# Twelve modulation pieces summed on three engines beside the first layer's projection, and the recurrence's preparation reordered

## The chip, the cores and the metric

The kernel runs on one core of one Trainium2 chip. The metric is the device time of one execution in microseconds; of the kernel before, three runs are known, with a median of 3143.65 us (3140.86 to 8241.34). The profile is of one further execution.

## What is computed

A two-layer hybrid diffusion backbone: 1024 latent tokens and 256 context tokens, width 1024, float32. Each layer first makes six modulation vectors for the latent and six for the context tokens out of two conditioning vectors:

```python
mod_l = silu(c)     @ w_ada[layer] + b_ada[layer]      # w_ada: (2, 1024, 6144)
mod_c = silu(c_ctx) @ w_ada[layer] + b_ada[layer]
sh1, sc1, g1, sh2, sc2, g2 = split(mod, 6)
h = rms_norm(x) * (1 + sc1) + sh1                      # both streams
layer 0:  z = h @ w_in; grouped attention beside a bidirectional chunkwise mLSTM; @ w_out
layer 1:  differential attention beside latent attention; @ w_out
each layer: x = x + g1 * mixer(h);  x = x + g2 * moe(rms_norm(x) * (1 + sc2) + sh2)
```

For the change only the products with `w_ada` matter. The matrix has 24 column pieces of 512 (NCHUNK), each 1024 x 512, 2 MB. A product of a vector with a piece is the sum over 1024 rows, that is over k = 0 to 7 (eight row blocks of 128, a row on each partition) and over the 128 partitions.

## The kernel before, in words

The stages follow one another; each is a block in which every engine and the DMA queue of SyncE has its own hand-written list, ordered by semaphores.

`modulation` makes the first four pieces (EARLY), which the first normalisation needs, on TensorE (`ada_product`, L152). `even_attend` and later stages make the last eight (LAST). The twelve between are the subject. Six of them (SUMMED = 6) are reduced over k, though not over the partitions, inside `even_project`; the other six are loaded whole, 2 MB each, in `even_mlstm`.

`even_project` (L366) walks ten tiles of 128 tokens, two tiles to a pair i, h = 0 or 1. A tile's order on TensorE (`tile`, L523): `rows` groups 0 and 1, `turn_qk` of the tile before, `rows` group 2, `transposes` of the tile after, `rows` group 3, `channels` in two halves. `turn_qk` waits for `x_sq` (ScalarE's squares at the end of the tile before) and for `z_dve`. `transposes` waits for the normalised x of the next tile (`xh_ready`) and for `qt_act` and `qt_dve`, the copies of the turned queries and keys out of PSUM; the latter is `k_out` on VectorE, which stands behind `rows_out`. VectorE's tile: `summed` half 0, `rows_out`, `k_out`, `norm_rope`, `modulate`, `summed` half 1, `channels_out`, `normalise` for the tile after next. ScalarE's tile: `rows_out`, `q_out`, `v_out`, `modulate`, `gate_out`, `channels_out`, `squares`.

`summed` (L679) takes one piece per tile, in tiles 1 to 6, with both conditioning vectors ("kinds"): SyncE loads the piece in two slabs of 1 MB into the last 512 columns of zT, VectorE multiplies each block k by a per-partition scalar and adds it to one of two accumulators in the last columns of qT, 16 instructions in all, where the two kinds alternate so that an instruction waits for the one before the last. `acc_store` writes both accumulators to `sum_dram`; the next piece waits for that store. GpSimd only fills `y_dram` with zeros (18.9 MB, L453), once the last part of the weights is in.

`even_mlstm` (L741) prepares the recurrence and then runs it. The preparation: SyncE loads eight units of up to 2 MB over four buffers (sums of pieces 0 to 3, three whole pieces, sums of 4 and 5, three whole pieces); TensorE reduces each (`product`), ScalarE copies it (`ada_out`), TensorE turns it (`turn`). Between them runs the chain of the gates: cumulated sums, an 18-step running maximum on one partition, two scans (L1131), exponentials; and the eight channel gates, a tanh on ScalarE (`gate`, L1029) and a product of 128x1280 on VectorE (`gated`, L1080), for which two buffers alternate. GpSimd stages each chunk of the recurrence (L902 to L908); its first staging waits for all eight channel gates, for the gate tables, for the rows loaded from `row_dram` and for the buffers that the loads of `w_ada` hold. TensorE's `scores` waits for that staging.

Of the kernel before, what the change touches and what calls it, by code (L numbers as in the profile page):

```python
# [144 lines left out]
SUMMED = 6  # L145
# [213 lines left out]

def modulation_of(g, layer, i, h, k):  # L360

    kind = 1 if isinstance(i, int) and i == 0 else 0
    return g.gain[:, layer, 0, k:k + 1, kind], g.mod[:, layer * 48 + V_SH1 * KD + k:layer * 48 + V_SH1 * KD + k + 1, kind]


def even_project(nc, g, A, L):  # L366
# [5 lines left out]
    with nc.cleanup_on_exit():  # L372
# [31 lines left out]
        acc = [L.qT[:, kind, T - 512:T] for kind in range(2)]  # L404
        slab_in, slab_used = [s("slab_in0"), s("slab_in1")], [s("slab_used0"), s("slab_used1")]
        acc_st = s("acc_st")
        c = Count(nc, "ep_dve_step")
        with nc.Block() as block:

            @block.sync  # L410
            def _(sp):
# [5 lines left out]
                def slab_load(n, half):  # L417
                    if n:
                        sp.wait_ge(slab_used[half], n)
                    col = (EARLY + n) * 512  # L420
                    sp.dma_start(slabs[:, 4 * half:4 * half + 4, :],
                                 A["w_ada"][0, half * 512:(half + 1) * 512, col:col + 512].rearrange("(k p) n -> p k n", p=P)).then_inc(slab_in[half], 16)

                def acc_store(n):
                    sp.wait_ge(slab_used[1], n + 1)
                    sp.dma_start(g.sum_dram[:, n, :, :], L.qT[:, 0:2, T - 512:T]).then_inc(acc_st, 16)
# [6 lines left out]
                x_load(1)  # L433
                for n in range(SUMMED):
                    if n + 1 < SUMMED:
                        slab_load(n + 1, 0)
                    x_load(n + 2)
                    acc_store(n)
                    if n + 1 < SUMMED:
                        slab_load(n + 1, 1)  # L440
                for n in range(SUMMED + 2, NTL):
                    x_load(n)
                sp.wait_ge(acc_st, 16 * SUMMED)

            @block.gpsimd
            def _(pool):
# [3 lines left out]
                pool.wait_ge(L.w_in[2], 16)  # L450
# [88 lines left out]
            def _(act):  # L539
# [38 lines left out]
                def channels_out(i, h, halves=(0, 1)):  # L578

                    if h == 0 and not place_of(i, h)[0] and not place_of(i, h)[1]:  # L580
                        act.wait_ge(slab_used[1], i * 2)
# [7 lines left out]
                def q_out(i, h):  # L589
                    if h == 0 and not place_of(i, h)[0] and not place_of(i, h)[1]:  # L590
                        act.wait_ge(acc_st, i * 32)
# [7 lines left out]
                def tile(i, h):  # L599
                    first, final, last, before, after = place_of(i, h)  # L600
                    rows_out(i, h)
                    if not first:
                        q_out(*before)
                    v_out(i, h)
                    if not last:
                        modulate(*after)
                    gate_out(i, h)
                    if last:
# [3 lines left out]
                    else:  # L612
                        channels_out(i, h)
                    if not final:
# [4 lines left out]
                walk_tiles(act, tile)  # L619
# [3 lines left out]
            def _(dve):  # L623
# [16 lines left out]
                def rows_out(i, h):  # L640
                    dve.wait_ge(r_done, i * 8 + 4 * h + 2)
                    dve.tensor_copy(qk[:, AW:QK], ps_r[:, 1, 0:AKW]).then_inc(*c.up())
# [36 lines left out]
                def summed(i, h, half):  # L679

                    n = i * 2 + h - 1
                    dve.wait_ge(slab_in[half], n * 16 + 16)
                    if half == 0 and not (isinstance(n, int) and n == 0):
                        dve.wait_ge(acc_st, n * 16)
                    for k in range(4 * half, 4 * half + 4):
                        for kind in range(2):
                            by = L.cs[:, k, kind:kind + 1]
# [2574 lines left out]
```

## Time and profile before

| | us |
|---|---|
| median of 3 runs | 3143.65 |
| the profiled execution | 3144.81 |
| its span, first to last instruction | 3142.90 |
| `modulation` | 0 to about 36 |
| `even_project` | about 36 to 447 |
| `even_mlstm`, preparation | 447 to 495 |
| recurrence | 495 to 600 |
| busy TensorE / VectorE / ScalarE / GpSimd | 2876.6 / 1481.4 / 1083.3 / 693.0 |

Times in a timeline are in us from the start of the span. A row has the start, the duration, the engine, the line of the kernel, the operation, output and inputs and the count of merged instructions; what stands in brackets is the engine's idle time before it and what ended that. PEclk is the granted TensorE clock, where 1.00 is 2.4 GHz and 0.50 is 1.2 GHz.

### The profile page before, as it was taken

The page shows a single profiled execution, that of the slowest core. Times are in us where ns is not written, and L with a number is a line of the kernel's source. Part 1 is how long each engine was busy: PE and PEld are TensorE (multiplying, and loading weights), DVE is VectorE, ACT ScalarE, POOL GpSimd, SP SyncE. Part 2 cuts the span into 40 slices and gives each one's busy share as a digit, 9 for nine tenths or more (in the row PEclk, how much of TensorE's full clock was granted, in tenths as well). Part 3 has the DMA queues.
Part 4 walks back from the last instruction along what each step waited for, and adds up shares of the span by engine and source line. Part 5 has one row for each costly group of instructions (what it writes and reads, how often), then busy time and mean ns, then how long its engine had stood idle before and what let it go on. Part 6 is the DMA issues. An engine that isn't in the chain of part 4 may idle for free. (4 is left out here: it accounts for less than half of the span.)

```text
span 3142.9 us, 72871 instructions
## 1 busy us (share of the span) xinstructions
PE 2876.6 (92%) x27771; PEld 1881.7 (60%) x27771; DVE 1481.4 (47%) x4244; ACT 1083.3 (34%) x2480; POOL 693.0 (22%) x929
## 2 busy tenths in 40 slices
PE   7999978899999689999987999899999959998895
PEld 4666657655544357776664555477776537785563
DVE  2666436755554522222224677666665342222223
ACT  1211224466611123333333443455553103332232
POOL 0000005798050033332221010000002013332233
PEclk8999988899999899999998999999999979998898
DMA  9822037432052499999984221200003459999997
GB/s 376 291 77 85 14 121 217 114 109 93 1 183 94 176 373 416 410 416 417 418 336 158 85 83 61 74 1 1 1 1 123 148 223 396 417 417 417 418 416 289
DMA packets 167396, 665.00 MB, mean 212 GB/s; under 512 B 25372, under 2 KB 37928, under 8 KB 117620
## 3 DMA queue, kind: packets, MB, share of 16 engines
q1 hardware_dynamic: 136736, 574.30, 47.1%
q0 software_dynamic: 19456, 56.67, 5.1%
q10 hardware_dynamic: 10964, 30.68, 2.6%
q8 instruction: 170, 2.79, 0.4%
q14 instruction: 70, 0.57, 0.1%
HBM read 581.98 MB, written 86.90 MB: 213 GB/s over the span
## 5 line engine op out<-in xcount | busy, mean ns | idle before, releaser
L2879 PE MATMUL ps_g<-w_ring,work 128*32 128x256 f32 x7328 | 434.7, 384 | 26.6 <-DMA w_ring<-in_w 15.1
L2966 DVE STREAM_TRANSPOSE work<-work 128x256 f32<-128x256 f32 x189 | 123.8, 655 | 660.9 <-PE ps_g L2879 638.1
L2932 ACT COPY work<-ps_y 32x256 f32<-32x256 f32 x760 | 275.8, 363 | 289.7 <-PE ps_y L2894 282.9
L2879 PEld LDWEIGHTS ps_g<-w_ring,work 128*32 128x32 f32 x7328 | 285.6, 111 | 144.9 <-issue 33.5
L2879 PE MATMUL ps_g<-w_early,work 128*32 128x256 f32 x4640 | 283.1, 390 | 30.8 <-DMA w_early<-in_w 19.8
L2004 PE MATMUL of_ps_r<-w_early,cat 128*128 128x512 f32 (+1 forms) x608 | 257.2, 579 | 1.6 <-ACT cat L2086 1.6
L486 PE MATMUL ps_r<-w,hT 128*128 128x512 f32 (+1 forms) x640 | 250.2, 547 | 1.5 <-ACT hT L556 1.5
L2879 PEld LDWEIGHTS ps_g<-w_early,work 128*32 128x32 f32 x4640 | 181.6, 112 | 111.7 <-issue 41.9
L2827 POOL DMA_INDIRECT work<-f_dram,ex_idx x200 | 204.5, 1023 | 171.4 <-POOL ex_idx L2824 170.6
L2894 PE MATMUL ps_y<-w_ring,work 128*32 128x256 f32 x3680 | 228.0, 382 | 3.9 <-ACT work L2932 3.4
L2926 ACT ACTIVATE work<-ps_g 128x128 f32<-128x128 f32 x192 | 53.2, 277 | 514.1 <-PE ps_g L2879 507.6
L2835 POOL COPY work<-work 128x256 f32<-128x256 f32 x192 | 76.6, 399 | 539.4 <-DVE work L2966 398.2
L2004 PEld LDWEIGHTS of_ps_r<-w_early,cat 128*128 128x128 f32 x608 | 115.2, 193 | 125.4 <-issue 123.2
L486 PEld LDWEIGHTS ps_r<-w,hT 128*128 128x128 f32 x640 | 120.5, 192 | 114.9 <-issue 107.5
L1655 PE MATMUL mo_ps_o<-mo_w,mo_cT 128*128 128x512 f32 x416 | 185.0, 596 | 1.4 <-DMA mo_w<-in_e_w_out 0.9
L2894 PEld LDWEIGHTS ps_y<-w_ring,work 128*32 128x32 f32 x3680 | 147.0, 111 | 61.2 <-ACT work L2932 4.3
L2466 DVE TENSOR_SCALAR_CACHE_REDUCE w_early<-oa_ps_s 128x512 f32<-128x512 f32 (+1 forms) x288 | 158.9, 598 | 20.3 <-PE oa_ps_s L2380 17.6
L2435 ACT ACTIVATE w_early<-w_early,oa_mins 128x1280 f32<-128x1280 f32 x96 | 131.0, 1364 | 66.1 <-DVE oa_mins L2472 66.1
L497 PEld LDWEIGHTS ps_ab<-hT,w 128*128 128x128 f32 x1280 | 144.6, 192 | 4.8 <-issue 4.8
L497 PE MATMUL ps_ab<-hT,w 128*128 128x128 f32 x1280 | 144.7, 275 | 0.0
L2894 PE MATMUL ps_y<-w_early,work 128*32 128x256 f32 x2304 | 144.6, 387 | 0.0
L1655 PEld LDWEIGHTS mo_ps_o<-mo_w,mo_cT 128*128 128x128 f32 x416 | 78.6, 191 | 99.7 <-issue 97.5
(509 smaller groups left out, 4441.0 us busy)
## 6 DMA issues: line engine op xcount, KB each, us to landing
w_ring<-in_w SPq DMA_DIRECT2D x232, 1024.0 KB, 25.3
w_early<-in_w SPq DMA_DIRECT2D x152, 1024.0 KB, 25.2
y_dram<-work ACTq DMA_DIRECT2D x190, 128.0 KB, 5.9
y_dram<-zeros POOLq DMA_DIRECT2D x4, 4608.0 KB, 26.8
ea_slab<-in_w_ada SPq DMA_DIRECT2D x64, 256.0 KB, 2.8
zT<-in_w_ada SPq DMA_DIRECT2D x12, 1024.0 KB, 6.5
f_dram<-mo_f SPq DMA_DIRECT2D x18, 512.0 KB, 2.9
w<-in_e_w_in SPq DMA_DIRECT2D x2, 4096.0 KB, 20.9
```

The lines of the kernel that those rows point to most:

```text
L486: mm = pe.matmul(ps_r[:, n, 0:cols[1] - cols[0]], hT[:, h, k, :], w[:, k, cols[0]:cols[1]], start=k == 0, stop=k == KD - 1)
L497: mm = pe.matmul(ps_ab[:, h, half, (cc % 4) * P:(cc % 4) * P + P], w[:, k, Z0 + cc * P:Z0 + (cc + 1) * P], hT[:, h, k, :], start=k == 0, s ...
L1655: mm = pe.matmul(ps_o[:, half * 512:(half + 1) * 512], row, w[:, k, half * 512:(half + 1) * 512], start=k == 0, stop=k == KD - 1)
L2004: mm = pe.matmul(ps_r[:, bank[m], 0:b - a], hT[:, n % 2, k, :], w[:, k, a:b], start=k == 0, stop=k == KD - 1)
L2435: act.activation(sx[:, n % 3, part, :], sx[:, n % 3, part, :], ACT.Exp, scale=-1.0, bias=mins[:, n % 3, part, 3:4], accum_out=sums[:, n % ...
L2466: dve.tensor_scalar(sx[:, n % 3, part, a:b], ps_s[:, k % 2, part, 0:b - a], -SCALE[units[n][1]], BIG, ALU.mult, ALU.min, accum_out=mins[:, ...
L2827: pool.indirect_dma_start(out=xg[:, at * 256:(at + 1) * 256], out_offset=None, in_=R.f_dram.rearrange("t (q d) -> (t q) d", q=QU), in_offs ...
L2835: pool.tensor_copy(xs, xg[:, at * 256:(at + 1) * 256]).then_inc(x_ready, 1)
L2879: mm = pe.matmul(ps_h[rows, :], xT[:, k * UNIT:(k + 1) * UNIT], w[:, :, kk * DE + n * P:kk * DE + (n + 1) * P], start=k == 0, stop=k == KD ...
L2894: mm = pe.matmul(ps_y[n * UNIT:(n + 1) * UNIT, :], hT[:, k * UNIT:(k + 1) * UNIT], w[:, kk, n * 256:(n + 1) * 256], start=k == 0, stop=k == 3)
L2932: w = act.copy(y[b * UNIT:(b + 1) * UNIT, n * 256:(n + 1) * 256], ps_y[n * UNIT:(n + 1) * UNIT, :])
L2966: dve.transpose(xT.rearrange("p (k t) -> p k t", k=KD), xs.rearrange("p (r k) -> p k r", k=KD)).then_inc(x_turned, 1)
```

## The change

All twelve middle pieces are summed in `even_project` (SUMMED = 12), two to a tile, in tiles 0 to 5. VectorE accumulates kind 0 alone, 8 instructions a piece, each of which waits for the one before. For kind 1 ScalarE multiplies (`weighed`, with a scale on each partition) into a ring of four products, which lie in the last columns of qT, kT and v, and GpSimd adds them up, seven adds a piece. ScalarE waits for GpSimd where the ring is full; GpSimd waits for the store of the sum before. The zeros of `y_dram` are now issued after GpSimd's last add. The second piece of tile 0 lies behind its `channels_out` and ahead of `squares` and `normalise`.

In `even_mlstm` three units of four summed pieces take the place of the eight. The preparation's order changes: the loads of the values come ahead of those of the rows, `gated(0)` and `gated(1)` move behind the scans, the clearing of `hb` is done at once (the tanh buffer that lay in it moves to `third`), and the copies of the products stand elsewhere among ScalarE's gates.

```diff
-SUMMED = 6
+SUMMED = 12
@@ even_project, SyncE
                 def slab_load(n, half):
                     if n:
-                        sp.wait_ge(slab_used[half], n)
+                        sp.wait_ge(used_dve[half], n)
+                        sp.wait_ge(product_made, 8 * n - 4 + 4 * half)
...
+                def sum_store(n):
+                    sp.wait_ge(used_dve[1], n + 1)
+                    sp.dma_start(g.sum_dram[:, n, 0, :], acc).then_inc(dve_st, 16)
+                    sp.wait_ge(product_added, 7 * n + 7)
+                    sp.dma_start(g.sum_dram[:, n, 1, :], acc_pool).then_inc(pool_st, 16)
...
                 for n in range(SUMMED):
+                    slab_load(n + 1, 0)
+                    slab_load(n + 1, 1)
+                    sum_store(n)
+                    if n % 2 == 0:
+                        x_load(n // 2 + 1)
@@ GpSimd
-                pool.wait_ge(L.w_in[2], 16)
+                for n in range(SUMMED):
+                    for k in range(1, 8):
+                        pool.wait_ge(product_made, 8 * n + k + 1)
+                        if n and k == 1:
+                            pool.wait_ge(pool_st, 16 * n)
+                        if n or k > 1:
+                            pool.wait_ge(product_added, 7 * n + k - 1)
+                        pool.tensor_tensor(acc_pool, product[0] if k == 1 else acc_pool, product[k % 4], ALU.add).then_inc(product_added, 1)
@@ ScalarE
+                def weighed(n, half):
+                    act.wait_ge(slab_in[half], n * 16 + 16)
+                    for k in range(4 * half, 4 * half + 4):
+                        if half:
+                            act.wait_ge(product_added, n * 7 + max(k - 4, 1))
+                        elif not (isinstance(n, int) and n == 0):
+                            act.wait_ge(product_added, n * 7 - 3 + k)
+                        act.activation(product[k % 4], slabs[:, k, :], ACT.Copy, scale=L.cs[:, k, 1:2]).then_inc(product_made, 1)
                 def tile(i, h):
+                    if sums and not first:
+                        weighed(n, 0)
                     rows_out(i, h)
                     if not first:
                         q_out(*before)
+                    if sums and not first:
+                        weighed(n, 1)
...
                     gate_out(i, h)
+                    if sums:
+                        for half in range(2):
+                            weighed(n if first else n + 1, half)
...
+                    if first:
+                        for half in range(2):
+                            weighed(1, half)
                     if not final:
                         squares(i + 1, h)
@@ VectorE
-                                dve.wait_ge(*c.but(1))
+                                dve.wait_ge(*c.now())
...
-                    if sums:
-                        summed(i, h, 0)
+                    if sums and not first:
+                        summed(n)
                     rows_out(i, h)
...
                     if sums:
-                        summed(i, h, 1)
+                        summed(n if first else n + 1)
                     channels_out(i, h)
+                    if first:
+                        summed(1)
@@ even_mlstm
+        units = [(4 * n, 4 * n + 4) for n in range(SUMMED // 4)]
@@ SyncE
-                        rows_in(0, step)
-                        rows_in(1, step)
-                        sp.wait_ge(ada_mm, LATE - 1)
                         for b in range(4):
                             values_in(b, tiles)
+                        sp.wait_ge(rows_out, 32)
+                        rows_in(0, step)
+                        rows_in(1, step)
@@ ScalarE
-                for cc in range(2, 8):
-                    gate(cc)
-                    if cc < 6:
-                        ada_out(cc)
-                for n in range(6, LATE):
-                    ada_out(n)
+                gate(2)
+                ada_out(2)
+                for cc in range(3, 8):
+                    gate(cc)
```

## Rows read from the trace of the kernel before

**Rows 1.** Windows: length, busy PE, PEld, DVE, ACT, POOL, then PEclk, DMA share, GB/s
```profile
130.00:170.00 40.00, 40.00 (x207) 27.80 (x206) 26.28 (x71) 7.95 (x19) 0.00 (x0) 1.00 0.36 123
...
447.00:500.00 53.00, 37.81 (x210) 17.53 (x211) 22.25 (x64) 19.22 (x27) 12.16 (x16) 0.69 0.99 346
```
**Rows 2.** Timeline of TensorE in tiles 1 to 3 of the projection
```profile
100.41 1.04 PE L469 MATMUL ps_ab<-consts_sb,x 128*128 128x128 f32 x8
...
122.44 10.70 PE L486 MATMUL ps_r<-w,hT 128*128 128x512 f32 x32
...
140.39 1.04 PE L469 MATMUL ps_ab<-consts_sb,x 128*128 128x128 f32 x8
...
162.42 10.70 PE L486 MATMUL ps_r<-w,hT 128*128 128x512 f32 x32
```
**Rows 3.** Timeline of VectorE in tile 2, which starts at 122.44
```profile
127.86 0.15 DVE L628 TENSOR_SCALAR xs<-xs 128x1 f32<-128x1 f32 x1 [1.27 <-ACT ps_ab L548]
...
130.10 0.88 DVE L689 TENSOR_SCALAR qT<-zT,cs 128x512 f32<-128x512 f32 x2
...
135.71 0.29 DVE L699 COPY kT<-ps_ab 128x128 f32 x1
...
145.80 5.38 DVE L692 SCALAR_TENSOR_TENSOR qT<-zT,cs,qT 128x512 f32<-128x512 f32 x8
157.20 0.30 DVE L667 COPY edges<-ps_ab 128x4 f32 x2 [6.02 <-ACT zT L585]
```
**Rows 4.** Timeline of ScalarE in tile 2
```profile
126.68 1.03 ACT L548 ACTIVATE ps_ab<-x 128x1024 f32<-128x1024 f32 x1 [2.54 <-DVE zT L675]
...
133.82 0.59 ACT L593 COPY qT<-ps_ab 128x512 f32 x1 [3.63 <-PE ps_ab L517]
```
**Rows 5.** GpSimd's adds of the same size in the attention stage, grouped by line
```profile
L1319 POOL TENSOR_TENSOR ea_slab<-ea_slab 128x512 f32<-128x512 f32 x56 | 71.3, 1273 | 4.7
```
**Rows 6.** Timeline of GpSimd at 883 us and in the recurrence
```profile
883.34 1.04 POOL L1610 TENSOR_TENSOR hb<-hb,mo_rs 128x512 f32<-128x512 f32 x1 [106.39 <-DVEq L1795]
884.46 3.20 POOL L1612 TENSOR_TENSOR hb<-hb,gbc 128x512 f32<-128x512 f32 x1
...
530.46 1.26 POOL L908 TENSOR_TENSOR ml_staging<-zT,ml_arena 128x512 f32<-128x512 f32 x1
```
**Rows 7.** Timeline of VectorE at 883 us and in the recurrence
```profile
883.36 3.18 DVE L1787 TENSOR_TENSOR mo_sq<-hb 128x2048 f32<-128x2048 f32 x1
...
530.55 1.18 DVE L1195 TENSOR_TENSOR ml_dn<-ml_dn,ml_cur 128x4 f32<-128x4 f32 x1
...
549.66 0.16 DVE L1195 TENSOR_TENSOR ml_dn<-ml_dn,ml_cur 128x4 f32<-128x4 f32 x1
```
**Rows 8.** DMA issues by line: KB each, median us from issue to landing
```profile
zT<-in_w_ada SPq DMA_DIRECT2D x12, 1024.0 KB, 6.5
...
sum_dram<-qT SPq DMA_DIRECT2D x6, 512.0 KB, 3.2
```
**Rows 9.** Windows of 2 us after stretches in which TensorE stood
```profile
44.00:46.00 2.00, 2.00 (x3) 0.67 (x2) 0.00 (x0) 0.00 (x0) 0.00 (x0) 0.54 0.99 397
...
456.00:458.00 2.00, 2.00 (x12) 0.44 (x12) 1.65 (x11) 0.00 (x0) 0.00 (x0) 0.50 1.04 396
...
492.00:494.00 2.00, 0.49 (x4) 0.20 (x8) 0.00 (x0) 0.00 (x0) 0.20 (x1) 0.74 1.01 267
```
**Rows 10.** Timeline of TensorE in the preparation
```profile
455.85 3.38 PE L924 MATMUL ml_ps_c<-ml_staging,ml_sel 128*32 128x512 f32 x16
...
493.51 3.32 PE L157 MATMUL ml_ps_c<-ml_arena,cs 128*32 128x512 f32 x16 [3.68 <-DMA ml_arena<-in_w_ada]
```
**Rows 11.** Timeline of VectorE in the preparation
```profile
459.47 0.15 DVE L1122 TENSOR_TENSOR ml_m_row<-ml_m_row 1x8 f32<-1x8 f32 x1
...
489.28 1.48 DVE L1080 SCALAR_TENSOR_TENSOR zT<-ml_spare,zT 128x1280 f32<-128x1280 f32 x1
```
**Rows 12.** Timeline of GpSimd: the first staging of the recurrence
```profile
494.97 0.20 POOL L902 COPY ml_cur<-ml_tab 128x16 f32<-128x16 f32 x1 [2.77 <-DMA ml_spare<-ml_rows]
```

More of the change, by code:

```diff
@@ L357, in place_of, with is_tile, has_sums @@
     return first, final, final and h == 1, (i, 0) if h else (i - 1, 1), (i + 1, 0) if h else (i, 1)
+def is_tile(i, h, n):
+    return isinstance(i, int) and i * 2 + h == n
+def has_sums(i, h):
+    return not (isinstance(i, int) and i * 2 + h >= SUMMED // 2)
 def modulation_of(g, layer, i, h, k):
@@ L578, in channels_out @@
                 def channels_out(i, h, halves=(0, 1)):
-                    if h == 0 and not place_of(i, h)[0] and not place_of(i, h)[1]:
-                        act.wait_ge(slab_used[1], i * 2)
+                    if is_tile(i, h, FREED):
+                        for half in range(2):
+                            act.wait_ge(used_dve[half], SUMMED)
                     for half in halves:
@@ L613, in tile @@
                         channels_out(i, h)
+                    if first:
+                        for half in range(2):
+                            weighed(1, half)
                     if not final:
@@ L618, in _ @@
                 modulate(0, 0)
-                walk_tiles(act, tile)
+                tile(0, 0)
+                tile(0, 1)
+                with act.Fori(0, FREED // 2 - 1) as j:
+                    tile(j + 1, 0)
+                    tile(j + 1, 1)
+                for i in range(FREED // 2, PAIRS):
+                    tile(i, 0)
+                    tile(i, 1)
                 act.wait_ge(vo_out, 16 * NT + 16)
@@ L702, in tile @@
                     first, final, last, before, after = place_of(i, h)
-                    sums = not first and not (isinstance(i, int) and i * 2 + h > SUMMED)
-                    if sums:
-                        summed(i, h, 0)
+                    sums, n = has_sums(i, h), i * 4 + 2 * h
+                    if sums and not first:
+                        summed(n)
                     rows_out(i, h)
@@ L765, in even_mlstm @@
         qs, ks, qa, tm = (staging[:, :, n, :, :] for n in range(4))
-        whole = EARLY + SUMMED
-        units = [("sums", 0, 4)] + [("whole", q) for q in range(whole, whole + 3)] + [("sums", 4, SUMMED)] + [("whole", q) for q in range(whole + 3, LAST[0])]
+        units = [(4 * n, 4 * n + 4) for n in range(SUMMED // 4)]
         LATE = len(units)
@@ L825, in _ @@
             def _(sp):
-                def load(n):
-                    if n >= len(wa):
-                        sp.wait_ge(ada_mm, n - len(wa) + 1)
-                    if units[n][0] == "sums":
-                        _, a, b = units[n]
-                        sp.dma_start(wa[buf(n)][:, 0:2 * (b - a), :], g.sum_dram[:, a:b, :, :].rearrange("p n w c -> p (n w) c")).then_inc(ada_in[buf(n)], 16)
-                    else:
-                        ada_load(sp, A, units[n][1], wa[buf(n)], ada_in[buf(n)])
-                for n in range(6):
-                    load(n)
+                for n, (a, b) in enumerate(units):
+                    sp.dma_start(wa[n], g.sum_dram[:, a:b, :, :].rearrange("p n w c -> p (n w) c")).then_inc(ada_in[n], 16)
                 sp.wait_ge(gd, 6)
@@ L841, in _ @@
                 sp.dma_start(row_dram[1].rearrange("d r t -> (d r) t"), ai_row).then_inc(rows_out, 16)
-                for n in range(6, LATE):
-                    load(n)
-                sp.wait_ge(rows_out, 32)
                 def rows_in(b, step):
@@ L964, in _ @@
                 pe.matmul(ps_s[:, 1, 0:P], g.ident[:, 0:1].to_broadcast([P, P]), ai_col, start=True, stop=True).then_inc(gp, 1)
+                turn(0)
+                product(2)
                 turn(1)
-                for n in range(3, LATE):
-                    product(n)
-                    turn(n - 1)
-                turn(LATE - 1)
+                turn(2)
                 def scores(u, b):
@@ L1137, in _ @@
                 dve.sem_inc(gd, 1)
+                gated(0)
                 dve.wait_ge(gp, 5)
```

132 lines of the change are left out of this document (58 added, 74 removed).

## The prediction

> **What bounds the kernel now.** I read the windows by stage first. In the projection TensorE is busy for 40.00 of 40.00 us at full clock, while VectorE has 26.3 us of work, ScalarE 8.0 and GpSimd none; in the preparation TensorE is busy 37.8 of 53 us at a mean clock of 0.69 and the DMA engines 0.99 of the time [rows 1]. So the projection is TensorE's and the preparation looks like the loads'. The second view is the timeline of each engine in one tile. TensorE starts a tile every 39.98 us (122.44, 162.42), and its transposes of the next x follow 17.95 us behind the start [rows 2]. Against these two marks everything that the change puts into a tile must be held. Third, the timelines of the preparation: the running maximum ends at 459.6 and the last channel gate at 490.8 [rows 11], GpSimd stages the first chunk at 494.97 [rows 12], and TensorE stands 3.7 us for the last whole piece [rows 10]. From GpSimd's start on, all later work only shifts.
>
> **The preparation: what is saved.** Before, 12 MB of whole pieces and 3 MB of sums went through four buffers; after, three units of 2.1 MB, each with a buffer of its own. At 396 GB/s [rows 9] from 448.5 the third lands at 448.5 + 3 x 5.3 = 464.4 (before, TensorE still waited for a load at 493.51). The chain that is left, step by step. The running maximum ends at 459.6 as before. Its turn into a column, a copy, two scans and their two ends took 2.2 us without the two channel gates that stood between them (2 x 1.48 less the little that they overlap); so the scans are done at 461.8. Then gated(0), 1.5, to 463.3; the small copies, 0.9, to 464.2; gated(1) to 465.7; copies and gated(2) to 467.6. ScalarE's gate(3) now stands behind the copy of the third unit: landing 464.4, TensorE free at about 466, a product of 3.4 us at half clock [rows 10], some 1.9 at full, copy 0.6, gate 1.3: 470 to 471.5. Five more products at a pitch of 1.45 (1.48 each on VectorE [rows 11], ScalarE one ahead) end at 477.2 to 478.7. The clearing of the tanh buffer (1.4 us) no longer stands between that and the staging. The rows of the tables are loaded behind 1 MB of values; their store goes out at 462.3, lands behind the third unit at about 467, and 1 MB of values and 1 MB of rows at 396 GB/s end at 473 to 476, ahead of the gates. GpSimd starts at 478.5 in place of 494.97: **16.5 us saved**, between 14 (rows land late, at 481) and 17.8 (full clock).
>
> **The projection without collisions.** Times in a tile are from its start on TensorE. The tile's first piece starts when x is normalised, 130.10 - 122.44 = 7.66 [rows 3]. Its eight chained instructions cost 0.48 and 7 x (0.745 + 0.035), 6.0 us; before, eight took 4.9. `rows_out` and `k_out` add 0.85: ready at 14.5, and the transposes want it at 17.95, a margin of 3.4 us. The second piece stands behind `modulate`, where 8 instructions took 5.38 and VectorE then waited 6.0 us for the channels [rows 3]. ScalarE gets 16 x 0.58 = 9.3 us beside its 8, and GpSimd 14 x 1.27 = 17.8 us [rows 5] of 40. Loads of 1 MB take 6.5 us and stores 3.2 [rows 8]; both pieces have over 8 us for it in tiles 2 to 5. The zeros, about 48 us at 396 GB/s, start at about 280 and are there long before 447. By busy time alone all of it lies beside TensorE. Only tile 1 is different: piece 1 stands behind `channels_out` of tile 0, so VectorE normalises x later, and piece 2 has to wait until the sum of piece 1 is stored. Without collisions VectorE ends piece 1 at 92.7, the 1 MB load and the store behind it land at 98 to 99, piece 2 takes 6.0, `k_out` 0.9: 105.2 against the transposes at 100.41 [rows 2], a stall of 4.8 us.
>
> **What the busy times hide: VectorE and GpSimd take turns.** In the trace VectorE's product of two SBUF tensors, 128x2048, starts at 883.36 beside GpSimd's 1.04 us product, and takes 3.18 us; GpSimd's next one starts at 884.46 and takes 3.20 us where 1.27 is its usual length: it ends 1.12 us behind VectorE's [rows 5 to 7]. In the recurrence a VectorE product of 128x4 lasts 1.18 us beside a GpSimd product (530.46 to 531.72, VectorE ends at 531.73), and 0.16 us when none runs [rows 6, 7]. So each stands until the other's instruction has ended, and they alternate. VectorE's multiply-adds here read two SBUF tensors (slab and accumulator), as do GpSimd's adds, so one pair costs 1.12 + 0.6 = 1.73 us, at most 1.27 + 0.78 = 2.05, in place of 0.78 for VectorE.
>
> The Trainium skill's page "SBUF — State Buffer" (section "Who interferes with whom") states this as a rule: a VectorE instruction with two SBUF inputs contends with a GpSimd instruction that reads SBUF, and the one that comes second blocks fully. It speaks against the split that this change makes; the trace agrees, with 1.18 against 0.16 us.
>
> *Tiles 2 to 5.* z_dve, where VectorE has copied the last channels of the tile before, is at 4.3. ScalarE's squares end at 5.4 (126.68 + 1.2 of its own tile) [rows 4], its products follow at 0.5 us each, and GpSimd's first add is ready at 6.8, in the midst of VectorE's normalisation. Adds 1 to 3 have their products at once; the fifth product stands behind the copy of the queries at 133.82, that is 11.4, so adds 4 to 7 come from 12.5 on [rows 4]. In order: add 1 to 8.05, add 2 to 9.2, the normalising product of x to 9.8, add 3 to 10.9, VectorE's first product to 11.3, multiply-adds 1 and 2 to 12.8, then four pairs to 19.7, the last multiply-add to 20.5, `rows_out` and `k_out` to 21.35. TensorE wants it at 17.95: a stall of 3.4 us. The second piece (behind `modulate` at about 31) pays the same seven collisions, 12.1 us in place of 6, and ends at about 45, which the wait for the channels (the channels' copies start at 34.8, [rows 3]) mostly hides; where it does not, the next tile starts 1.4 us later in its own time and the stall is 4.8. Such a stand also costs clock: the window of 44 to 46 us has 0.54, though TensorE had been at work since 40.1 without a stop, and the stand before 493.51, 3.7 us, was followed by 3.3 us at half clock [rows 9, 10]. Half clock for 3 to 6 us is 1.5 to 2.9 us. I take 5.4 us a tile, **21.6 us** for four. Bounds: 3.4 (no clock lost) and 11 (pairs of 2.05, full 8 us stall and 2.9 of clock), 13.6 and 44 us.
>
> *Tile 1.* Piece 1 alternates with its seven adds and ends at 98.3, not 92.7; load and store behind it land at 104 to 106; piece 2 with its seven pairs takes 0.45 + 12.1 and ends at about 117.6, `k_out` at 118.5: 18 us behind 100.41, and 2.9 of clock. **21 us**; bounds 16 and 25.
>
> **The sum.** +21.6 + 21 - 16.5 = +26 us on the profiled execution's 3144.8, so 3171; on the median of the runs shown, 1.2 us lower, 3170. A measurement of this kernel can tell about 2%, 63 us, from no change.
>
> **Rivals.**
> 1. *The two engines do not collide on these operands.* Then tile 1 costs 4.8 + 1.7 of clock and nothing else: 3143.7 + 6.5 - 16.5 = 3134, faster. For it: nothing in the trace but the durations of GpSimd's adds in the attention stage (1.27 throughout), where VectorE reads PSUM. Against it: both rows above. It decides at VectorE's first piece of a tile: below 9.4 us with no stall, above it TensorE waits. 15%.
> 2. *Collisions at the upper bounds.* Pairs of 2.05, both pieces of a tile late, so each tile starts with z_dve at 7.7 and stalls 8.3 us and loses 2.9 in clock: 4 x 11.2 + 25 - 16.5 = +53, 3197. For it: VectorE's busy 28 plus 17.8 us of adds, plus waits for squares and channels, come near 48 a tile. Against it: the overlaps of 0.13 us in the rows. 17%.
> 3. *The stage's gain is not there:* the gates' chain is bound by something that the loads hid, such as the rows landing behind the values at 486. Then 8 us are saved: 3178. Against it: 6 MB in place of 15. 5%.
> 4. Slower by over 63 us: with the queries' copy on ScalarE held by GpSimd as well, tile after tile. 4%.
>
> **Chances and range.** The forecast (net +10 to +42) has 59%. The range goes from rival 1's 3134 to rival 2's 3197. The likeliest case alone spans 3152 to 3186. Faster by over 2%: 1%; within 2%: 95%; slower: 4%.
>
> **What would show it.** Right: in tiles 2 to 5 TensorE stands 3 to 5 us ahead of L469's transposes for kT's copy, and once about 18 us in tile 1; VectorE's multiply-adds of 128x512 last 1.1 to 1.9 us in the mean instead of 0.745, and windows of 40 us show a granted clock below 1.00; the projection ends near 447 + 42 = 489 and the first staging comes 31 us after that, not 48. Wrong: multiply-adds of 0.75 us with GpSimd's adds beside them (rival 1), or a tile of 48 us and more (rival 2). The preparation is wrong where GpSimd's first staging waits for loaded rows, not for the last gate.

## The result and the profile after

| | before | after |
|---|---|---|
| median of 5 runs each, on one chip, us | 3140.86 | 3168.65 |
| the profiled execution's span, us | 3142.9 | 3165.3 |
| mean period of tiles 2 to 5, us | 39.98 | 45.87 |
| tile 1, us | 39.98 | 58.48 |
| start of `even_mlstm`, us | 447.41 | 490.88 |
| from there to the first staging, us | 47.56 | 30.18 |

The ratio after to before is 1.0094 with a 95% interval of 1.0072 to 1.0116: about 28 us slower, clear of noise, and within 2%. One of the five runs of the kernel before took 8241.34 us; its cause is not known and it is left out of the ratio. The projection grew by 43.5 us and the preparation gave 17.4 back; at the first staging the changed kernel is 26.1 us behind (494.97 in [rows 12] against 521.06). The later stages of these two profiled executions differ by 4 us the other way, which is less than the runs of one kernel differ among themselves (3163.05 to 3175.39).

What TensorE waits for in the projection, grouped by the instruction that waits (us in total, times, longest). The kernel before had no wait of this kind:

```profile
PE ps_ab L497 <- DVE kT L757: 30.5, 5, 16.3
```

L497 are the transposes of the next x (L469 before), L757 is `k_out` on VectorE. There are five stands (a stand is a stretch in which TensorE waits), one in each of tiles 1 to 5. TensorE's timeline in tiles 1 and 2:

```profile
83.57 10.70 PE L514 MATMUL ps_r<-w,hT 128*128 128x512 f32 x32
...
118.00 1.94 PE L497 MATMUL ps_ab<-consts_sb,x 128*128 128x128 f32 x8 [16.32 <-DVE kT L757]
119.73 8.19 PE L514 MATMUL ps_r<-w,hT 128*128 128x512 f32 x16
...
142.05 10.70 PE L514 MATMUL ps_r<-w,hT 128*128 128x512 f32 x32
...
163.53 1.94 PE L497 MATMUL ps_ab<-consts_sb,x 128*128 128x128 f32 x8 [3.37 <-DVE kT L757]
165.27 7.61 PE L514 MATMUL ps_r<-w,hT 128*128 128x512 f32 x16
```

Compare with [rows 2]. The transposes take 1.94 us in place of 1.04, and the 16 matmuls behind them, 7.03 us at full clock, take 7.6 to 8.2 here and up to 9.0 in tiles 3 to 5: the stand is paid a second time in clock. The stands of tiles 3 to 5 are 3.59, 3.62 and 3.62 us. By windows of 40 us (busy PE, PEld, DVE, ACT, POOL, then granted clock, DMA share, GB/s):

```profile
90.00:130.00 40.00, 23.68 (x84) 14.07 (x83) 33.65 (x53) 11.61 (x22) 17.97 (x12) 0.79 0.47 151
130.00:170.00 40.00, 36.63 (x181) 25.44 (x180) 32.89 (x61) 16.48 (x32) 19.87 (x14) 0.96 0.46 151
...
290.00:330.00 40.00, 36.38 (x181) 24.77 (x180) 32.23 (x62) 13.97 (x27) 21.86 (x15) 0.91 0.38 127
```

In [rows 1] the window from 130 to 170 us showed 40.00 us of TensorE at 1.00, and VectorE 26.28. Why VectorE is late is seen where its timeline and GpSimd's lie beside each other. VectorE's timeline in tile 2, which starts at 142.05:

```profile
150.05 0.75 DVE L688 TENSOR_SCALAR x<-x,xs 128x1024 f32<-128x1024 f32 x1
150.72 1.49 DVE L747 TENSOR_SCALAR qT<-zT,cs 128x512 f32<-128x512 f32 x1
152.25 4.28 DVE L750 SCALAR_TENSOR_TENSOR qT<-zT,cs,qT 128x512 f32<-128x512 f32 x3
156.75 5.59 DVE L750 SCALAR_TENSOR_TENSOR qT<-zT,cs,qT 128x512 f32<-128x512 f32 x4 [0.21 <-DVE qT L750]
162.56 0.29 DVE L701 COPY qk<-ps_r 128x128 f32<-128x128 f32 x1 [0.23 <-DVE qT L750]
...
163.10 0.29 DVE L757 COPY kT<-ps_ab 128x128 f32 x1
```

And GpSimd's timeline in the same stretch:

```profile
148.74 1.27 POOL L477 TENSOR_TENSOR qT<-qT 128x512 f32<-128x512 f32 x1 [7.34 <-ACT qT L633]
150.15 1.78 POOL L477 TENSOR_TENSOR qT<-qT,kT 128x512 f32<-128x512 f32 x1
152.07 1.27 POOL L477 TENSOR_TENSOR qT<-qT,v 128x512 f32<-128x512 f32 x1
154.71 2.94 POOL L477 TENSOR_TENSOR qT<-qT 128x512 f32<-128x512 f32 x2 [1.37 <-ACT qT L633]
157.80 1.53 POOL L477 TENSOR_TENSOR qT<-qT,kT 128x512 f32<-128x512 f32 x1
159.47 1.53 POOL L477 TENSOR_TENSOR qT<-qT,v 128x512 f32<-128x512 f32 x1
```

Seven multiply-adds take 9.87 us where 7 x 0.75 would be 5.2. GpSimd's adds, spaced 1.67 us, and VectorE's multiply-adds go in turns; when the adds end at 161.0 VectorE is nearly done too, and `k_out` is copied at 163.10, 21.05 us into the tile, where the transposes wanted it at 17.95.

### The profile page after: what moved, and what is told of

Read it like the earlier page. It is cut to its first block and busy times, and to the rows that moved or that the text cites. A ratio compares the mean times of both kernels' runs of the same rounds, so it can differ in the third digit from the quotient of the medians.

```text
span 3165.3 us, 72995 instructions
## 1 busy us (share of the span) xinstructions
PE 2862.0 (90%) x27659; PEld 1862.9 (59%) x27659; DVE 1543.3 (49%) x4244; ACT 1143.3 (36%) x2571; POOL 814.4 (26%) x1012
## 5 line engine op out<-in xcount | busy, mean ns | idle before, releaser
L2907 PE MATMUL ps_g<-w_ring,work 128*32 128x256 f32 x7328 | 429.9, 383 | 27.1 <-DMA w_ring<-in_w 16.5
L2907 PEld LDWEIGHTS ps_g<-w_ring,work 128*32 128x32 f32 x7328 | 278.6, 111 | 151.5 <-issue 34.2
L514 PE MATMUL ps_r<-w,hT 128*128 128x512 f32 (+1 forms) x640 | 256.6, 558 | 1.5 <-ACT hT L584 1.5
```

What stands on the lines that cost most here:

```text
L514: mm = pe.matmul(ps_r[:, n, 0:cols[1] - cols[0]], hT[:, h, k, :], w[:, k, cols[0]:cols[1]], start=k == 0, stop=k == KD - 1)
L2907: mm = pe.matmul(ps_h[rows, :], xT[:, k * UNIT:(k + 1) * UNIT], w[:, :, kk * DE + n * P:kk * DE + (n + 1) * P], start=k == 0, stop=k == KD ...
```

## Experiments

The theory from here on is *turn-taking*: a VectorE instruction with SBUF operands and a GpSimd add exclude each other, so that handing the second kind to GpSimd lengthens VectorE's own half. The rivals are named with each run. Each ratio is to the kernel before in the same session. VectorE's multiply-adds from 83 to 330 us, which are those of all pieces but the first, as one group (count, busy us, mean ns, idle before) are used several times. In the changed kernel:

```profile
L750 DVE SCALAR_TENSOR_TENSOR qT<-zT,cs,qT 128x512 f32<-128x512 f32 x77 | 101.6, 1320 | 4.8 <-DVE qT L750 2.5
```

And in e6_vector_both below, where VectorE does both kinds:

```profile
L726 DVE SCALAR_TENSOR_TENSOR qT<-zT,cs,qT 128x512 f32<-128x512 f32 x154 | 103.9, 746 | 2.6 <-DVE qT L726 2.6
```

**1. GpSimd only writes.**

```diff
-pool.tensor_tensor(acc_pool, product[0] if k == 1 else acc_pool, product[k % 4], ALU.add).then_inc(product_added, 1)
+pool.memset(acc_pool, 0.0).then_inc(blanked, 1)
+pool.wait_ge(blanked, 7 * n + k)
+pool.memset(acc_pool, 0.0).then_inc(product_added, 1)
```

> The changed kernel with each of GpSimd's 84 adds replaced by two chained memsets of 128x512, about 1.2 us together, in the same place and behind the same semaphores; kind 1 of the twelve pieces is left out by it. Turn-taking theory (only a GpSimd instruction that reads SBUF holds up VectorE's multiply-adds): the multiply-adds of 128x512 are back at 0.74 us and a pitch of 0.78, the stands of 3.4 to 3.6 us before the transposes in tiles 2 to 5 are gone, the one in tile 1 falls from 16.3 to about 5 us; 36 us less than the changed kernel, about 3133. Rival (any work of GpSimd at that time, or the longer way over ScalarE and the stores, is the cause): the stands stay at 3.4 to 3.6 and 16 us, about 3169.

Measured 3135.22 us, ratio 0.9961 (0.9947 to 0.9975). GpSimd works as often as before and nearly as long, two memsets of 0.53 us for one add, but reads nothing:

```profile
L753 DVE SCALAR_TENSOR_TENSOR qT<-zT,cs,qT 128x512 f32<-128x512 f32 x77 | 57.9, 752 | 4.8 <-DVE qT L753 2.5
```

752 ns in place of 1320. The stands in tiles 2 to 5 are gone (starts at 132.27, 172.26, 212.24 and so on, 39.98 apart); tile 1 keeps one of 6.06 us. So the number of GpSimd's instructions and the semaphore waits are not the cause: the adds themselves are. A memset differs from an add in that it reads nothing, but also in that it computes nothing. A pair of rows of the changed kernel's recurrence parts the two: there a VectorE product of 128x4, which takes 0.16 us alone, starts within a GpSimd copy and ends with it, at 539.8 both; a copy reads but computes nothing. VectorE:

```profile
539.32 0.46 DVE L1223 TENSOR_TENSOR ml_dn<-ml_dn,ml_cur 128x4 f32<-128x4 f32 x1
```

GpSimd:

```profile
539.12 0.65 POOL L948 COPY ml_staging<-zT 128x512 f32 x1
```

So it is the reading that holds VectorE up. The preparation again took 30.18 us. Its start lies 9.9 us later than in the kernel before: 8.3 in tile 1 with its clock, and 1.5 ahead of tile 1. Tile 1 is taken up in experiments 6 and 8.

**2. `k_out` ahead of the piece.** The collisions stay, but what TensorE waits for is no longer behind them.

```diff
+rows_out(i, h)
+if not first:
+    k_out(*before)
 if sums and not first:
     summed(n)
-rows_out(i, h)
-if not first:
-    k_out(*before)
```

> The changed kernel with one thing moved: in a tile VectorE does rows_out and k_out before its first piece, not behind it. Theory (the collisions cost only because the keys' copy stands behind eight multiply-adds): no stand before the transposes in any of tiles 1 to 5; tile 1 instead makes the next tile wait 3 to 4 us for VectorE's half of the modulated x, since its first piece starts only at 105.6; VectorE's z_dve moves to about 9.3 in the next tile, right at the 10.55 at which TensorE wants the squares, so tiles of 40 to 42 us; about 3135 to 3146. Rival (VectorE's throughput is the bound: 28 us of work, 14 adds' worth of waits and its waits for squares and channels do not fit in 40 us): tiles stay at 45 us with the stand elsewhere, about 3160.

Measured 3149.67 us, ratio 1.0020 (1.0010 to 1.0029), 19 us below the changed kernel but above the expected range. The stand only moved. TensorE's waits:

```profile
PE ps_ab L544 <- ACT ps_ab L576: 9.4, 5, 2.7
PE ps_r L514 <- DVE hT L694: 6.3, 1, 6.3
```

The tile after tile 1 waits 6.3 us for VectorE's half of the modulated x, where 3 to 4 had been expected. L576 are ScalarE's squares of the x after next, which wait for VectorE's `channels_out`. So once `k_out` is out of the way the next thing that VectorE's backlog reaches is late, tile after tile, by 0.84 to 2.73 us. The order was part of the cost, VectorE's lengthened work the rest: the truth lies between the two forecasts of this run.

**3. ScalarE's second products later** (on top of experiment 2), between the halves of `channels_out`, so that GpSimd's adds should miss VectorE's second piece.

```diff
-if sums:
+if sums and first:
     for half in range(2):
-        weighed(n if first else n + 1, half)
+        weighed(n, half)
+if sums and not first:
+    channels_out(i, h, (0,))
+    for half in range(2):
+        weighed(n + 1, half)
+    channels_out(i, h, (1,))
...
```

> As e2_kout_first, and ScalarE makes the products of a tile's second piece between its two halves of channels_out, so that GpSimd adds them while VectorE reads PSUM. Theory: the second piece's multiply-adds are back at 0.78 us pitch (6 us for eight), its seven adds meet only channels_out, which reads one SBUF tensor; tiles 2 to 5 at 40.0 us with no stand, one stand of 3 to 5 us behind tile 1; about 3128 to 3134, 7 to 13 us below the kernel before. Rival (later products delay the squares, on which TensorE's turn of the queries waits): a stand of 1 to 4 us ahead of the turning of the queries in each tile, 3135 to 3150.

Measured 3145.82 us, ratio 1.0003 (0.9994 to 1.0013). A miss, 12 us above the expected range; its interval overlaps that of experiment 2. The adds came later, but VectorE was late enough to meet them. The second piece of tile 3, which runs over into tile 4 (TensorE starts it at 216.74), in VectorE's timeline:

```profile
212.40 4.11 DVE L755 SCALAR_TENSOR_TENSOR qT<-zT,cs,qT 128x512 f32<-128x512 f32 x3
217.08 6.13 DVE L755 SCALAR_TENSOR_TENSOR qT<-zT,cs,qT 128x512 f32<-128x512 f32 x4 [0.57 <-DVE qT L755]
```

And GpSimd's:

```profile
216.10 1.53 POOL L477 TENSOR_TENSOR qT<-qT,v 128x512 f32<-128x512 f32 x1
217.78 3.21 POOL L477 TENSOR_TENSOR qT<-qT 128x512 f32<-128x512 f32 x2
```

Stands for the squares of 1.71, 2.66, 2.54 and 2.19 us stayed. The time and these stands are those that the rival of this run gave, but not by its mechanism: ScalarE was not late with the squares by its own products, it stood idle 8.82 us ahead of them, waiting for VectorE's `channels_out`. ScalarE's timeline:

```profile
228.60 1.03 ACT L576 ACTIVATE ps_ab<-x 128x1024 f32<-128x1024 f32 x1 [8.82 <-DVE zT L739]
```

Where VectorE has two pieces of work in every tile, moving the adds finds no stretch without it.

**4. The gates back ahead of the scans,** the reordering of the preparation undone in one point.

```diff
 dve.sem_inc(gd, 1)
+gated(0)
+gated(1)
 dve.wait_ge(gp, 4)
```

> The changed kernel with gated(0) and gated(1) back in front of the scans in the recurrence's preparation. My reckoning of the preparation: the scans end 2.2 to 3 us later, the tables later by as much, and the last channel gate, on which GpSimd's first staging waits, by 1 to 2 us, as two products of VectorE are out of the way later: the first staging 31.5 us behind the stage's start in place of 30.2. Rival (the order is worth nothing since ScalarE's third copy bounds the gates): 30.2 as before.

One run, 3172.1 us. Its stage starts at 488.84 and stages first at 521.34, that is 32.50 us later against 30.18: this part of the reordering is worth 2.3 us, about twice the 1.3 expected. A single run cannot show that in the total; the trace does.

**5. The whole pieces of the preparation before, cut to an eighth.** The kernel before, in which each of the six whole pieces loads 256 KB in place of 2 MB; the products read that one block eight times. Both loads of sums stay.

```diff
-ada_load(sp, A, units[n][1], wa[buf(n)], ada_in[buf(n)])
+layer, col = units[n][1] // (NCHUNK // 2), units[n][1] % (NCHUNK // 2) * 512
+sp.dma_start(wa[buf(n)][:, 0, :], A["w_ada"][layer, 0:P, col:col + 512]).then_inc(ada_in[buf(n)], 16)
...
```

> The kernel before, but the five whole pieces of the recurrence's preparation load 256 KB each in place of 2 MB and their products read that one block eight times (this part of the computation is left out). The theory that the loads set the preparation's end: the first staging comes 30 to 37 us after the stage's start in place of 47.6, total 3126 to 3133. Rival: the gates' chain with the five pieces' copies between them sets it: 43 to 48 us, total 3138 to 3143.

One run, 3128.3 us. The stage starts at 446.43 and stages first at 480.16: 33.7 us after the start in place of 47.56, with every product, copy and turn of the eight units still made. So the loads set the end of the preparation before, as [rows 1] suggested with their share of 0.99, and not the copies between ScalarE's gates. The 33.7 us are still 3.5 more than the changed kernel's 30.18, which leaves room for the 2.3 us of experiment 4.

**6. VectorE makes both kinds.** ScalarE's products and GpSimd's adds are taken out, the twelve pieces in six tiles stay.

```diff
...
-by = L.cs[:, k, 0:1]
+for kind in range(2):
+    by, to = L.cs[:, k, kind:kind + 1], (acc, acc_pool)[kind]
...
-m = dve.scalar_tensor_tensor(out=acc, in0=slabs[:, k, :], scalar=by, in1=acc, op0=ALU.mult, op1=ALU.add)
+m = dve.scalar_tensor_tensor(out=to, in0=slabs[:, k, :], scalar=by, in1=to, op0=ALU.mult, op1=ALU.add)
```

> All twelve pieces stay in six tiles, but VectorE makes both kinds of each (alternating, as the kernel before did: 16 instructions, about 10.3 us a piece); ScalarE's products and GpSimd's adds are gone. Turn-taking theory: VectorE's own part of a piece took 10.9 us with GpSimd's adds in its way, so handing it the other half costs it nothing, and what GpSimd delayed besides (the normalisation, the rope) comes back: the stands before the transposes in tiles 2 to 5 shrink from 3.6 to 1.5-3 us, tile 1's from 16.3 to 13-16, the total is 3145 to 3165. Rival: the offload did relieve VectorE and the stands come from something else (the copy of the queries on ScalarE, the loads): then 16 instructions more on VectorE make the tiles longer than the changed kernel's, 3170 to 3200.

Measured 3152.38 us, ratio 1.0036 (1.0024 to 1.0048): 16 us faster than the changed kernel, with twice the instructions on VectorE. This is the answer to what the offload bought: the two group lines at the head of this section say 77 multiply-adds in 101.6 us against 154 in 103.9 us. Beside the 57.9 us of experiment 1, GpSimd's adds lengthened VectorE's own half by 43.7 us, and making the other half as well costs 46.0. Five stands remain; those of tiles 3 and 5 are 1.63 us each, and in TensorE's timeline those of tiles 1, 2 and 4:

```profile
116.34 1.94 PE L485 MATMUL ps_ab<-consts_sb,x 128*128 128x128 f32 x8 [15.13 <-DVE kT L733]
159.91 1.06 PE L485 MATMUL ps_ab<-consts_sb,x 128*128 128x128 f32 x8 [1.23 <-DVE kT L733]
246.13 1.10 PE L485 MATMUL ps_ab<-consts_sb,x 128*128 128x128 f32 x8 [4.25 <-DVE kT L733]
```

Tile 1's stand hardly shrank (15.13 for 16.32): a piece of tiles 0 and 1 costs VectorE 10.5 us here and 11.3 in the changed kernel, and tile 1's piece still has to wait 4.68 us for the store of the piece before. Experiment 8 takes that up, and experiment 9 the longer stand of tile 4.

**7. The same with `k_out` first** (the edit of experiment 2 on top of 6).

> The same with rows_out and k_out ahead of the tile's first piece. VectorE's own work in a tile is then about 15.5 + 21 = 37 us of 40 with no turns taken. Turn-taking theory: the stands for the squares (0.8 to 2.7 us in e2_kout_first) shrink below 1.5 us or vanish, and the total is 3132 to 3145, below e2_kout_first's 3149.7. Rival: e2_kout_first's stands come from the order of VectorE's work alone (the piece stands between k_out and the rest), whoever does the second kind: 3147 to 3155.

Measured 3139.95 us, ratio 0.9992 (0.9982 to 1.0003), 10 us below e2_kout_first, whose order it shares. Two stands for the squares are left (8.9 us, the longest 5.7) and one of 2.2 us for hT, where five and one stood. The total is as the theory had it, but the stands for the squares were to shrink below 1.5 us, and the longer one, 5.68 us, stands right behind tile 1. With no turns taken two pieces a tile nearly fit beside TensorE.

**8. The pieces moved by one** (on top of experiment 7): one in tile 0, two in each of tiles 1 to 5, one in tile 6.

```diff
-return not (isinstance(i, int) and i * 2 + h >= SUMMED // 2)
+return not (isinstance(i, int) and i * 2 + h > SUMMED // 2)
...
-sums, n = has_sums(i, h), i * 4 + 2 * h
+sums, n = has_sums(i, h), i * 4 + 2 * h - 1
...
-if sums:
-    summed(n if first else n + 1)
+if sums and not is_tile(i, h, FREED):
+    summed(n + 1)
...
-if first:
-    summed(1)
...
```

> e7_both_kout_first with the pieces moved by one: one in tile 0, two each in tiles 1 to 5, one in tile 6 (rows_out and k_out ahead of each tile's first piece, VectorE makes both kinds). What is left in e7_both_kout_first beside the time of the stage before is tile 1: 2.2 us for hT and 5.7 us for the squares, with the half clock behind them, some 10 us, and 3.2 us in a later tile. If that comes from the second piece in tile 0, it goes: the recurrence's preparation starts at 450 to 456 (463.05 in e7_both_kout_first, 447.4 in the kernel before), its first staging comes 29 to 30 us later, and the total is 3126 to 3134, the first version below the kernel before. Rival: two pieces a tile leave VectorE too little slack wherever they stand, and the stands move to tiles 2 to 5: 3136 to 3145.

Measured 3128.9 us, ratio 0.9952 (0.9939 to 0.9966): faster than either kernel. Tile 1 runs in 39.99 us (81.62 to 121.61): the waits behind it that experiment 7 had, 2.20 us for hT and 5.68 for the squares, are gone, and only the place of the pieces was changed, with the order of the loads of x that goes with it. One stand is left, in tile 5:

```profile
255.68 1.09 PE L534 MATMUL ps_ab<-consts_sb,sq 128*128 128x128 f32 x4 [3.17 <-ACT ps_ab L566]
```

VectorE's timeline a tile earlier has what looked like its origin, a gap in which the engine waited for nothing that the profile shows:

```profile
213.78 0.75 DVE L667 TENSOR_SCALAR x<-x,xs 128x1024 f32<-128x1024 f32 x1
216.86 0.29 DVE L678 COPY qk<-ps_r 128x128 f32<-128x128 f32 x1 [2.33 <-issue]
```

**9. VectorE's loop over tiles 2 to 5 written out** (on top of experiment 8).

```diff
-with dve.Fori(0, turns) as j:
-    c.turn(j, 2 * (1 + RSTD_1) + 2 * (2 + HEAD_NORM_N + ROPE_N) + 2 * (4 * KD + 2))
-    tile(j + 1, 0)
-    tile(j + 1, 1)
-c.turned(turns)
-for i in range(turns + 1, PAIRS):
+for i in range(1, PAIRS):
```

> e8_shifted with VectorE's loop over tiles 2 to 5 written out (the other engines keep theirs). In e8_shifted one stand is left, 3.17 us for the squares in tile 5, 1.1 us of slow transposes and half clock behind it. VectorE issued nothing for 2.33 us at 214.5, in tile 4, where its loop turns back; with 37 us of work in 40 that delay is still there a tile later. If the turn of the loop is the cause, the stand goes: preparation's start at 447 to 449 (453.07 in e8_shifted), total 3121 to 3127. Rival: VectorE is late in tile 5 because 37 us of work with its waits do not fit 40: the stand stays at 2 to 3.5 us, and the written-out code may cost fetches of its own: 3127 to 3133.

Measured 3124.58 us, ratio 0.9941 (0.9928 to 0.9954). The gap and the stand are gone, and TensorE's tiles from 121.69 to 281.63 are 39.98 us apart. The intervals of experiments 8 and 9 overlap, so this step is shown by the traces and not by the totals. VectorE's timeline at the same place of the work, without a pause:

```profile
211.67 0.75 DVE L667 TENSOR_SCALAR x<-x,xs 128x1024 f32<-128x1024 f32 x1
212.40 0.29 DVE L678 COPY qk<-ps_r 128x128 f32<-128x128 f32 x1
```

So the gap needs the loop; but the loop does not always bring it. The kernel before and experiments 5 to 8 have such a gap of 2.33 to 2.64 us where VectorE goes from tile 3 to tile 4. The changed kernel and experiments 1 to 4 turn a loop over the same tiles at the same place and have none. What makes the difference no run shows. VectorE's timeline in the kernel before:

```profile
213.18 0.88 DVE L689 TENSOR_SCALAR qT<-zT,cs 128x512 f32<-128x512 f32 x2 [2.50 <-issue]
```

And in the changed kernel:

```profile
241.91 0.75 DVE L688 TENSOR_SCALAR x<-x,xs 128x1024 f32<-128x1024 f32 x1
242.59 1.48 DVE L747 TENSOR_SCALAR qT<-zT,cs 128x512 f32<-128x512 f32 x1
```

GpSimd's timeline, the start of `even_mlstm` and the first staging:

```profile
446.67 1.06 POOL L893 MEMSET ml_tab<- 128x1152 f32 x1 [90.24 <-POOLq L3130]
477.33 0.20 POOL L917 COPY ml_cur<-ml_tab 128x16 f32<-128x16 f32 x1 [23.51 <-DVE zT L1082]
```

The stage starts where it did before (446.67 against 447.41) and the first staging comes 30.66 us later in place of 47.56: all twelve pieces are summed under the projection, and the whole saving of the preparation reaches the total: the medians are 17.4 us apart (3141.97 and 3124.58).

## Why the prediction was right, step by step

| term | forecast, us | measured, us |
|---|---|---|
| tile 1: stand and clock | 18 + 2.9 = 21 | 16.32 + 2.2 = 18.5 |
| tiles 2 to 5: stands | 4 x 3.4 = 13.6 | 3.37 + 3.59 + 3.62 + 3.62 = 14.2 |
| tiles 2 to 5: clock | 8.0 | 9.4 |
| start of tile 1 later | 0 | 1.1 |
| later tiles | 0 | 0.3 |
| the preparation | -16.5 | -17.4 |
| sum | +26 | +26.1 at the first staging |
| median | 3170 | 3168.65 |

The clock terms are what a tile's period has over 39.98 beyond its stand: 44.96, 46.47, 45.44 and 46.61 us for tiles 2 to 5, together 23.6 over.

The mechanism was right: the turn-taking, the copy of the keys behind it, the clock and the load-bound preparation all came as forecast. That the sum agrees to a tenth of a us is luck. The terms were off by -2.5, +2.0, +1.1, +0.3 and -0.9 us, which cancel, and the two profiled executions are 22 us apart over their whole span, the medians 28. Two small slips of the forecast moved nothing: the net of +10 stands beside a lower end of 3152, which is +8, and the stall of tiles 2 to 5 is bounded by 11 us in one place and 11.2 in another.

**Preparation.** The chain held at each mark, in us from the stage's start. Running maximum done: forecast 459.6 - 447.4 = 12.2, measured 12.2. Scans 14.4 and 14.1. The fourth gate on VectorE, behind the third unit's copy, 22.6 to 24.1 and 23.0. Last gate done 29.8 to 31.3 and 30.1. The forecast's 478.5, which is 31.1 us behind the start, lies near the upper end of its range, where the third unit's product is made at half clock (3.4 us). It ran at full clock, in 1.92, and GpSimd followed the last gate at once, at 30.18. Its first staging was released by the gate and not by a load, the mark set for this step. VectorE's last gate in its timeline:

```profile
519.50 1.49 DVE L1111 SCALAR_TENSOR_TENSOR zT<-ml_spare,zT 128x1280 f32<-128x1280 f32 x1
```

GpSimd's first staging:

```profile
521.06 0.20 POOL L946 COPY ml_cur<-ml_tab 128x16 f32<-128x16 f32 x1 [23.03 <-DVE zT L1111]
```

Experiment 5 shows the premise, that the loads set the stage before; experiment 4 puts the reordering's own part at 2.3 us of the 17.4.

**Tiles 2 to 5.** In the tile's own time: first add of GpSimd forecast 6.8, measured 6.7; fourth add 12.5 and 12.7; end of the last multiply-add 20.5 and 20.3; `k_out` copied 21.35 and 21.34. The pair of an add and a multiply-add was put at 1.73 us; GpSimd's alternating adds start 1.67 us apart. A detail was wrong without moving the end: VectorE's first product, which has only one tensor to read, was costed free of collision at some 0.4 us. It took 1.49 in the first piece of these tiles, but x was normalised earlier, so that it began at 8.7 where 10.9 had been reckoned. The second piece was hidden, as forecast, but it was costed too dear: 9.0 to 9.6 us in place of 12.1, since ScalarE's products for it came late enough that the first three multiply-adds met no add (in tile 2 they take 2.33 us from 173.69 on, and GpSimd's first add starts at 175.68). It ended at 40.7 in place of 45 in tile 2's own time. The clock cost a little more than forecast, 1.6 to 3.0 us a tile in place of 2.0.

**Tile 1.** Piece 1 (of tile 0) ended at 99.0 (forecast 98.3), the store behind it let VectorE start at 105.64 (104 to 106), `k_out` was done at 117.9 (118.5). The stand came out 1.7 us shorter because the tile itself began 1.1 us later, which the forecast did not have, and `k_out` was done 0.6 earlier. Over the experiments the tile's start lay anywhere between 81.47 and 83.96; experiment 4, whose projection is that of the changed kernel, has 81.89 against 83.57. So the shift is not shown to come from the change: one kernel's executions differ by as much. The sentence that without collisions tile 1 would stand 4.8 us is borne out by experiment 1 with 6.06. But experiment 6 shows what that split hid: with both kinds on VectorE, and no collisions, the tile stands 15.13. So while a piece costs VectorE 10 us or more, by turns or by its own work, the second piece in tile 0 is what makes VectorE late in tile 1. With `k_out` first, in experiment 7, the stand before the transposes was gone but 2.20 and 5.68 us came behind it; with that piece moved as well, in experiment 8, there was none.

**The rivals.** Rival 1 (no collision, 3134) is what experiment 1 measured when the reading was taken away, 3135.22: its price was right, its condition false. Rival 2 (pairs of 2.05 us, both pieces late) did not come: the pair was 1.67. Rival 3 fell with the 17.4 us. Of rival 4 (slower by over 63 us) nothing came; ScalarE's products ran longer than reckoned (below), but did not reach the end of the tile.

The forecast said what the split costs, and nowhere asked what the alternative costs, VectorE doing all of it. Its own numbers had the answer: 12.1 us for a piece with collisions, against 4.9 + 5.4 = 10.3 us for the sixteen instructions of both kinds in the kernel before [rows 3]. Measured, a piece with GpSimd's adds took VectorE 11.3 to 11.6 us as the first of its tile and 9.0 to 9.6 as the second of tiles 2 to 5, and with both kinds on VectorE 10.5.

## What to carry to other kernels

Work handed from VectorE to GpSimd was no relief here, where both read tensors in SBUF: before handing such work over, compare what an add beside it costs VectorE (a pair every 1.67 us in place of 0.78, so 0.9) with what VectorE would need for it itself (0.75). Before a second engine is brought in, put the consumer's copy ahead of the filler work, place the filler where no transfer chain binds it (here one tile later), and look in the trace for a gap at the turn of a loop; here these three and the offload undone brought the medians from 3168.65 to 3124.58 us, with the kernel before at 3140.86 and 3141.97 beside them. When a stand is removed, look at once for the next thing that the same engine delivers late, as in experiment 2.

## What the runs showed of the hardware

- Twice the multiply-adds in the same time: 154 alone took 103.9 us, 77 beside GpSimd's adds 101.6. The adds, 1.27 us alone, lasted 1.53 while alternating.
- A GpSimd instruction that only writes did not hold up VectorE's instructions with two tensors in SBUF: beside GpSimd's memsets the multiply-adds kept 752 ns. This agrees with the Trainium skill, page "SBUF — State Buffer", section "Who interferes with whom", by which a VectorE instruction with two SBUF inputs contends with a GpSimd instruction that reads SBUF and not with one that only writes.
- The product of one tensor, 128x512 from SBUF to SBUF, was held by both kinds: 0.48 us alone, 1.49 beside the adds, and 0.83 beside a memset, which itself took 0.96 in place of 0.53. The same section says that an instruction in VectorE's two-port mode contends with GpSimd, and that `tensor_scalar` can be in that mode; these rows agree, though no row shows the mode itself. VectorE's product in e1_memset:

```profile
139.94 0.83 DVE L750 TENSOR_SCALAR qT<-zT,cs 128x512 f32<-128x512 f32 x1
```

And GpSimd's memset beside it:

```profile
139.53 0.96 POOL L480 MEMSET qT<- 128x512 f32 x1
```

- With one of its two tensors in PSUM a VectorE product was not held: in the recurrence of the changed kernel L1205 (128x512, one input in PSUM, one in SBUF) took 679 to 692 ns in all 20 cases, such as 0.68 us at 538.27 beside no product of GpSimd and 0.69 at 542.19 within a GpSimd product of 1.28.
- VectorE does not always get its turn after one instruction. The adds of the change wait for each other by semaphore; where GpSimd's instructions follow without a wait, a VectorE product of 128x4 (0.16 us alone) stood through two copies and two products of GpSimd. VectorE in the changed kernel:

```profile
532.29 3.66 DVE L1223 TENSOR_TENSOR ml_dn<-ml_dn,ml_cur 128x4 f32<-128x4 f32 x1
```

And the last of GpSimd's four:

```profile
534.67 1.26 POOL L952 TENSOR_TENSOR ml_staging<-zT,ml_arena 128x512 f32<-128x512 f32 x1
```

- ScalarE's products from SBUF to SBUF took 0.71 us each, one every 0.62, where 0.5 to 0.58 had been reckoned; its copy of the queries from PSUM, of the same size, 0.59.
- The shortest stands of TensorE cost little more than themselves: in e6_vector_both one of 1.23 us left the transposes at 1.06 us and the period at 41.41, 1.43 over 39.98; the stand of 3.37 us in the changed kernel cost 4.98.
- VectorE issued nothing for 2.33 us (e8_shifted) where its loop turned back. With 26 us of work in a tile of 40, in the kernel before, a gap of 2.50 cost TensorE nothing; with 37 it cost TensorE 3.17 us and its clock a tile later, about 6 us of the stage's start in all (453.07 to 446.67).
